# Two transformer blocks on one core: the dilated layers' values as products of 512 columns

## The chip, the cores and the metric

The kernel runs on one core of one Trainium2 chip. The metric is the device time of one execution in microseconds; several executions are timed and the median is compared. Every matrix product is made in three parts in a 32-bit format: an operand is split into a high part and a low part, and high x high, low x high and high x low are added up in PSUM.

## The reference

The input is 512 tokens of 1024 features. `first_block` runs two layers, `second_block` one.

```python
def first_block(x, ...):
    for layer in range(2):
        h = rms_norm(x, norm_g[layer])
        p = h @ w_in[layer]
        c_q, c_kv, k_r, gate_a, dil_qkv, gate_b = jnp.split(p, split_points, axis=-1)
        a = mla_attention(c_q, c_kv, k_r, ...) * jax.nn.silu(gate_a)
        b = dilated_attention(dil_qkv, cos_d, sin_d) * jax.nn.silu(gate_b)
        x = x + jnp.concatenate([a, b], axis=-1) @ w_out[layer]
    return rms_norm(x, final_g)
```

`dil_qkv` holds queries, keys and values (8 heads of 64) for three groups with dilations 1, 4 and 16. Each group attends within a band of its strided tokens; the three outputs are merged with weights from their sums of exponentials. `second_block` is a feed-forward stage (1024 to 2816 and back), a mixer (recurrence, sliding-window attention, gates), and a second feed-forward stage, each followed by a norm and a residual.

## The kernel before, in words

**Weight chunks.** All weights pass through one pipeline of chunks of 2048 columns per partition, two slots deep. SP loads a chunk into `WS` (`load`, L860), ScalarE copies it to its high part `WH` (`hi_of_chunk`), VectorE subtracts to get the low part `WL` (`lo_of_chunk`), TensorE multiplies. A slot of `WH` and `WL` comes free when the products of the chunk two before it are done. During an attention the chunk after next is split by the Pool engine instead (`split_in`). `make_plan` (L232) lists chunks and results in order and gives every wait its count; the order itself is written out by hand in each engine's program.

**Two forms of product.** `feature_major` (L1015) holds 128 x 128 of a weight and streams 512 tokens: 8 k-steps x 2 tiles x 3 parts = 48 products of 512 columns a chunk. `token_major` (L1053) holds 128 tokens' features and streams a weight's row of 256 columns, so that the result has tokens on the partitions: 8 x 4 x 3 = 96 products of 256 columns. The values (`v`) of the dilated attention are made in this form. They are 1536 columns wide: three groups g, two halves hh of the heads, 256 columns each; so six chunks in each layer.

**One layer.** For each half hh the chunks come in `DILATED_ORDER` (L225): q0, k0, v0, q1, k1, q2, k2, v1, and then the attention with eight items, for which `attention` (L1111) issues the scores of two items, then a filler chunk (here v2, on banks 6 and 7), then for every item scores, turning of the probabilities, and the products with values. ScalarE copies a values chunk out of PSUM in four blocks, scaled by the tokens' inverse norm (`from_token_major`, L1605). Group 0's values must be regrouped by residue of the token number. The Pool engine's queue writes them to DRAM and loads them back in 12 pieces (L926 to L938); value products of the first item wait for `v0_in`. The last turning and value products of an attention (`rest`) are issued between the first steps of the next chunk.

After the second half's attention come the gate chunks gb0 and gb1, then in0, in1, in2 (the latent columns) and ga0, ga1 (gates of the other attention). Between these chunks `weights_spread` (L1359) turns the merging weights of four pairs of heads with eight transposes each; VectorE makes the weights (`merge`, L2250, `weights_copy`, L2269) and applies them (`combine`, L2276).

**The start.** The input is loaded in four parts, each followed by the matching parts of chunks 0 and 1. TensorE turns each input part into a pair of banks (`input_turned`), ScalarE copies it to `X` and from `X` makes the high part with the gain (L1830, L1603), VectorE the low part (L2128); products of the first two chunks follow part by part (`first_step`). Between, `idle_products` (L1082) multiplies constants, so that TensorE is not idle.

**The passages.** After the first feed-forward stage and after the mixer, a norm over the whole result is needed before anything else: sums of squares (`norm_sum`, L1078), the root on ScalarE, the reciprocal on VectorE, a spread by four transposes (`norm_spread`, L1101), then residual and split. Three idle products stand before the spread, seven behind it (each two instructions of 128 columns at L1085).

Of the kernel before, what the change touches and what calls it, by code (L numbers as in the profile page):

```python
# [25 lines left out]
F32 = mybir.dt.float32  # L26
# [198 lines left out]
DILATED_ORDER = [("q", 0), ("k", 0), ("v", 0), ("q", 1), ("k", 1), ("q", 2), ("k", 2), ("v", 1)]  # L225
# [6 lines left out]
def make_plan():  # L232
# [3 lines left out]
    for L in range(DEPTH):  # L236
        pl.split(("x", L), KD)
        pl.norm(("x", L), KD)
        for hh in range(2):
            for w, g in DILATED_ORDER:  # L240
                if (w, g, hh) == ("v", 0, 0) or (w, g) == ("v", 1):
                    pl.aside((w, L, hh, g), "a", 3)
                    pl.add_chunk((w, L, hh, g), KD, CW, (w, L, hh, g))
                    continue
                pl.gemm((w, L, hh, g), "a" if w == "v" else "d")
                if w != "v":
                    pl.rope[w, L, hh, g] = len(pl.rope) + 1
            pl.attention(("dil", L, hh), [dict(kind="dil", L=L, t=t, j=2 * hh + jj, hh=hh, jj=jj)
                                          for jj in range(2) for t in range(NT)],
                         lambda: pl.filler(("v", L, hh, 2), "a"))  # L250
        for j in range(2):
            pl.gemm(("gb", L, j), "d")
        for j in range(3):
            pl.aside(("wb", L, j), "d", 3)
            pl.gemm(("in", L, j), "d")
# [91 lines left out]
def build_program(nc, a, out):  # L347
# [3 lines left out]
    with ctx:  # L351
# [76 lines left out]
        VD = ARENA[:, 6144:6144 + 3072].rearrange("p (g t c) -> p g t c", g=GROUPS, t=NT)  # L428
        OUN = view(9216, 4, 2, S)
# [85 lines left out]
        first_in = [sem(f"first_in{f}") for f in range(4)]  # L515
# [57 lines left out]
        v0_in = sem("v0_in")  # L573
        rls_ready = sem("rls_ready")
# [48 lines left out]
        def chunk_source(key):  # L623
            kind = key[0]
            if kind in ("in", "ga", "q", "k", "v", "gb", "uq", "ukv", "wo"):
                L = key[1]
                w = a["w_in"][L]
                if kind == "in":
                    return cols(w, key[2] * CW)
                if kind == "ga":  # L630
                    return cols(w, COL_GA + key[2] * CW)
                if kind in "qkv":
                    hh, g = key[2:]
                    return cols(w, COL_DIL + (3 * g + "qkv".index(kind)) * HEADS * HD + hh * CW)
# [15 lines left out]
        def landing(c):  # L650

            return 16 * (c // 2)

        def staged(c, columns):

            return THIRD[:, 0:columns] if c == 2 else WS[:, c % 2, 0:columns]

# [74 lines left out]
        def value_products(it):  # L732
# [10 lines left out]
            elif it["kind"] == "dil":  # L743
                for block in range(NT):
                    for b in range(2):
# [4 lines left out]
                        got.append((dst, 4 * b + block, VD[:, g, tile, h * HD:(h + 1) * HD],  # L750
# [44 lines left out]
        filler_of.update({("dil", L, hh): ("v", L, hh, 2) for L in range(DEPTH) for hh in range(2)})  # L795
# [37 lines left out]
        def _(sp):  # L833
            for f in range(4):
# [3 lines left out]
                for c in range(2):  # L838
                    sp.dma_start(slot(WS, c, KD, CW)[:, 2 * f:2 * f + 2, :],
                                 chunk_source(pl.chunks[c][0])[:, 2 * f:2 * f + 2, :]).then_inc(first_in[f], 16)  # L840
# [2008 lines left out]
```

## Time and profile before

| | us |
|---|---|
| median of 3 runs | 2117.63 |
| lowest, highest | 2116.81, 2117.83 |
| the profiled execution | 2117.32 |
| its span, first to last instruction | 2115.5 |
| TensorE busy in the span | 2099.6 |
| VectorE, ScalarE, Pool busy | 1135.1, 804.9, 121.8 |

The profile's rows come from one execution. Times on the left of a timeline row count from the span's start; a row of the timeline gives start, duration, engine, source line, operation, output and input, shape and count, and in brackets the idle time before it and what ended it. Products overlap in TensorE, so a product's own duration (0.28 or 0.39 us) is longer than the time from one start to the next.

### The profile page before, as it was taken

The page shows a single profiled execution, that of the slowest core. Times are in us where ns is not written, and L with a number is a line of the kernel's source. Part 1 is how long each engine was busy: PE and PEld are TensorE (multiplying, and loading weights), DVE is VectorE, ACT ScalarE, POOL GpSimd, SP SyncE. Part 2 cuts the span into 40 slices and gives each one's busy share as a digit, 9 for nine tenths or more (in the row PEclk, how much of TensorE's full clock was granted, in tenths as well). Part 3 has the DMA queues.
Part 4 walks back from the last instruction along what each step waited for, and adds up shares of the span by engine and source line. Part 5 has one row for each costly group of instructions (what it writes and reads, how often), then busy time and mean ns, then how long its engine had stood idle before and what let it go on. Part 6 is the DMA issues. An engine that isn't in the chain of part 4 may idle for free.

```text
span 2115.5 us, 28304 instructions
## 1 busy us (share of the span) xinstructions
PE 2099.6 (99%) x11655; PEld 1745.4 (83%) x11655; DVE 1135.1 (54%) x1543; ACT 804.9 (38%) x1296; POOL 121.8 (6%) x113
## 2 busy tenths in 40 slices
PE   8999999999999999999999999999999999999998
PEld 7888988788988887788888888787788888888886
DVE  6565557746555557664444435875643445333333
ACT  5152425723332526543122226463632245222223
POOL 0111100201001100200000002001000001000001
PEclk9999999999999999999999999999999999999999
DMA  5414212123323121123332224234023322333221
GB/s 189 120 41 120 81 60 82 41 61 101 100 58 105 59 79 64 41 80 99 99 99 86 99 95 149 86 116 138 12 90 100 100 80 90 99 99 99 100 99 60
DMA packets 158097, 189.03 MB, mean 89 GB/s; under 512 B 4194, under 2 KB 147876, under 8 KB 157860
## 3 DMA queue, kind: packets, MB, share of 16 engines
q1 hardware_dynamic: 153204, 174.41, 26.1%
q0 software_dynamic: 4608, 13.00, 2.0%
q8 instruction: 80, 1.31, 0.3%
q14 instruction: 29, 0.24, 0.0%
q10 hardware_dynamic: 176, 0.07, 0.0%
HBM read 182.20 MB, written 7.36 MB: 90 GB/s over the span
## 4 chain that ended last, share of the span: by engine, by line
PE 97%; DVE 1%; ACT 1%; issue 0%; DMA 0%; SPq 0%; DVEq 0%; ACTq 0%
PE PS L997 27%; PE PS L999 26%; PE PS L998 26%; PE PS L1126 5%; PE PS L1169 4%; PE PS L1138 4%; PE PS L1009 1%; PE PS L1005 1%; PE PS L1006 1%; PE PS L1078 0%; PE PS L1295 0%; DMA ARENA<-in_x 0%; PE PS L1369 0%; PE PS L1101 0%; DVE WL L2067 0%
## 5 line engine op out<-in xcount | busy, mean ns | idle before, releaser
L997 PE MATMUL PS<-UH,WH 128*128 128x512 f32 x1632 | 641.2, 393 | 0.1
L999 PE MATMUL PS<-UH,WL 128*128 128x512 f32 x1632 | 635.6, 389 | 0.0
L998 PE MATMUL PS<-UL,WH 128*128 128x512 f32 x1632 | 635.4, 389 | 0.0
L1566 ACT ACTIVATE WH<-WS 128x2048 fp32r<-128x2048 f32 x98 | 187.9, 1917 | 609.1 <-PE PS L999 587.6
L997 PEld LDWEIGHTS PS<-UH,WH 128*128 128x128 f32 x1632 | 306.4, 188 | 68.1 <-issue 6.1
L999 PEld LDWEIGHTS PS<-UH,WL 128*128 128x128 f32 x1632 | 306.3, 188 | 64.7
L998 PEld LDWEIGHTS PS<-UL,WH 128*128 128x128 f32 x1632 | 306.5, 188 | 61.5
L2067 DVE TENSOR_TENSOR WL<-WS,WH 128x2048 fp32r<-128x2048 f32 x98 | 224.3, 2289 | 234.4 <-ACT WH L1566 234.4
L2356 DVE TENSOR_TENSOR WL<-WS,WH 128x2048 fp32r<-128x2048 f32 x44 | 100.7, 2288 | 150.8 <-ACT WH L1739 150.8
L1739 ACT ACTIVATE WH<-WS 128x2048 fp32r<-128x2048 f32 x44 | 84.4, 1918 | 248.9 <-PE PS L999 246.6
L997 PE MATMUL PS<-WH,UH 128*128 128x256 f32 x416 | 118.3, 284 | 0.2 <-DVE WL L2067 0.2
L998 PE MATMUL PS<-WL,UH 128*128 128x256 f32 x416 | 117.7, 283 | 0.0
L999 PE MATMUL PS<-WH,UL 128*128 128x256 f32 x416 | 117.7, 283 | 0.0
L1138 PE MATMUL PS<-IDN,PR 128*128 128x128 f32 x624 | 85.7, 277 | 1.3 <-DVE PT L2212 0.3
L1169 PE MATMUL PS<-PT,ARENA 128*64 128x128 f32 x1248 | 85.8, 279 | 0.0
L1138 PEld LDWEIGHTS PS<-IDN,PR 128*128 128x128 f32 x624 | 69.6, 140 | 16.0 <-issue 7.2
L997 PEld LDWEIGHTS PS<-WH,UH 128*128 128x128 f32 x416 | 79.8, 192 | 2.2 <-DVE ARENA L2136 0.8
L998 PEld LDWEIGHTS PS<-WL,UH 128*128 128x128 f32 x416 | 79.8, 192 | 0.3
L999 PEld LDWEIGHTS PS<-WH,UL 128*128 128x128 f32 x416 | 79.8, 192 | 0.0
L1169 PEld LDWEIGHTS PS<-PT,ARENA 128*64 128x64 f32 x1248 | 66.5, 136 | 14.3 <-issue 14.3
L2212 DVE COPY PT<-PS 128x512 f32<-128x512 f32 (+1 forms) x80 | 53.7, 672 | 33.5 <-PE PS L1138 33.5
L997 PE MATMUL PS<-HH,WH 128*128 128x512 f32 x176 | 68.5, 389 | 0.0
(320 smaller groups left out, 3091.4 us busy)
## 6 DMA issues: line engine op xcount, KB each, us to landing
WS<-in_ffn_w SPq DMA_DIRECT2D x66, 1024.0 KB, 5.2
WS<-in_w_in SPq DMA_DIRECT2D x61, 1024.0 KB, 5.4
WS<-in_w_out SPq DMA_DIRECT2D x8, 1024.0 KB, 5.2
WS<-in_w_gate SPq DMA_DIRECT2D x8, 1024.0 KB, 5.3
WS<-in_w_attn_out SPq DMA_DIRECT2D x4, 1024.0 KB, 5.5
WS<-in_w_lru_out SPq DMA_DIRECT2D x4, 1024.0 KB, 5.4
WS<-in_w_o SPq DMA_DIRECT2D x4, 1024.0 KB, 5.1
bias_skewed<-bias_rows POOLq DMA_DIRECT2D x1, 3072.0 KB, 13.4
```

The source lines that it names most:

```text
L997: nc.tensor.matmul(dst, sh, mh, start=start, stop=False, skip_group_check=True)
L998: nc.tensor.matmul(dst, sh, ml, start=False, stop=False, skip_group_check=True)
L999: return nc.tensor.matmul(dst, sl, mh, start=False, stop=stop, skip_group_check=True)
L1005: nc.tensor.matmul(dst, sh, mh, start=start, stop=False, skip_group_check=True)
L1126: last[b] = nc.tensor.matmul(acc[:, c0:c0 + w], q, k, start=start, stop=True, skip_group_check=True)
L1138: last = nc.tensor.transpose(bank(4 + b)[:, k * P:(k + 1) * P], PR[:, n % 2, b * S + k * P:b * S + (k + 1) * P], IDN[:, :])
L1169: last = nc.tensor.matmul(dst, v, PT[:, n % 2, k * P:(k + 1) * P], start=start, stop=stop, skip_group_check=True)
L1566: nc.scalar.activation(WH[:, c % 2, 0:kt * n], staged(c, kt * n), ACT.Copy).then_inc(w_hi, 1)
L1739: nc.scalar.activation(WH[:, c % 2, :], WS[:, c % 2, :], ACT.Copy).then_inc(w_hi, 1)
L2067: tt(WL[:, c % 2, 0:kt * n], staged(c, kt * n), WH[:, c % 2, 0:kt * n].bitcast(F32), ALU.subtract).then_inc(w_split, 1)
L2212: nc.vector.tensor_copy(used_half(it, PT[:, n % 2, 0:S]), used_half(it, bank(4))).then_inc(pt_dve, 1)
L2356: tt(WL[:, c % 2, :], WS[:, c % 2, :], WH[:, c % 2, :].bitcast(F32), ALU.subtract).then_inc(w_split, 1)
```

## The change

- **Values.** The six values chunks of a layer become six half-row chunks of the same size: 4 of the 8 k-steps, 512 columns, namely two blocks of 256 side by side. `vv` is groups 0 and 1 of one half hh, `vw` is group 2 of both halves; each has two chunks (part 0 and part 1 of the k-steps). `value_half` streams 512 columns into banks 4 to 7, one bank for each tile of tokens, in the order 2, 3, 0, 1; the accumulation runs over both chunks. ScalarE's `values_out` copies eight blocks after the second. Group 2 of the second half is kept in a place of its own, `VDB`.
- **Order.** First half: q0, k0, vv, vv, q1, k1, q2, k2, vw, vw. Second half: q0, k0, q1, k1, q2, k2, vv, vv. The filler of the dilated attentions is a gate chunk (gb1, then gb0) instead of a values chunk; VectorE takes it out by a multiply.
- **Round trip.** In the first half Pool's queue does it as before, in the second half SP's queue (`by_residues`), once blocks (0, 0) to (0, 3) are copied.
- **Behind the second half.** in0 follows at once, with `rest` between its steps; the spreads of in1 and in2 stand between their steps.
- **Start.** One idle run of 7 on constants before any load; ScalarE makes the high part straight from the turned tile, VectorE the low part too, and `X` is copied afterwards. The weight parts of chunks 0 and 1 have a semaphore and a place each. Input part 1 is turned after the first two steps of chunk 0, not before them.
- **Passages.** Idle products of 512 columns, 4 before the spread and 9 behind it. The norm of the second layer's input is summed one step later.

```diff
-DILATED_ORDER = [("q", 0), ("k", 0), ("v", 0), ("q", 1), ("k", 1), ("q", 2), ("k", 2), ("v", 1)]
+DILATED_ORDER = ([("q", 0), ("k", 0), ("vv", 0), ("vv", 1), ("q", 1), ("k", 1), ("q", 2), ("k", 2),
+                  ("vw", 0), ("vw", 1)],
+                 [("q", 0), ("k", 0), ("q", 1), ("k", 1), ("q", 2), ("k", 2), ("vv", 0), ("vv", 1)])
...
+            def by_residues(L):
+                sp.wait_ge(w0_here, L + 1)
+                sp.dma_start(VSCR.rearrange("(i r) c -> i r c", r=NT), VRES).then_inc(w0_out, 16)
+                sp.wait_ge(w0_out, 16 * (L + 1))
+                for r in range(NT):
+                    of_r = VSCR.rearrange("(i r) c -> r i c", r=NT)[r]
+                    sp.dma_start(VD[32 * r:32 * r + 32, 0, 0:3, :], ...).then_inc(w0_in, 16)
+                    for x in range(2):
+                        sp.dma_start(VD[p0:p0 + 16, 0, 3, :], ...).then_inc(w0_in, 16)
...
+                if key[0] == "gb" and key[2] == 0:
+                    load(c, chunk_source(pl.chunks[c][0]))
+                    c += 1
+                    load(c, chunk_source(pl.chunks[c][0]))
+                    c += 1
+                    by_residues(key[1])
...
+            def value_half(w, L, hh, part):
...
+                for k in range(KD // 2):
+                    for t in (2, 3, 0, 1):
...
+                        tok = slice(t * P, (t + 1) * P)
+                        row = KD // 2 * part + k
+                        last = three(bank(4 + t), UH[:, row, tok], UL[:, row, tok], slot(WH, c, KD // 2, 2 * CW)[:, k, :],
+                                     slot(WL, c, KD // 2, 2 * CW)[:, k, :], row == 0, row == KD - 1)
+                last.then_inc(acc_ready, 1)
...
+            def wide_idle_products(n, of):
+                for _ in range(n):
+                    nc.tensor.matmul(bank(5), of[:, 0:P], of, start=True, stop=True, skip_group_check=True)
...
+                    if n == n0 and kind == "dil":
+                        pe.wait_ge(act_out, pl.act_out["vv" if it["hh"] else "vw", it["L"], it["hh"], "all"])
...
-                    idle_products(3, bank(5)[:, 0:P])
+                    wide_idle_products(4, HH[:, 0, 0, :])
                     norm_spread((f, "post"))
-                    idle_products(7, bank(5)[:, 0:P])
+                    wide_idle_products(9, HH[:, 0, 0, :])
...
+            pe.wait_ge(const_ok, 1)
+            idle_products(7, bank(3)[:, 0:P], ONES)
...
             input_turned(0)
             idle_products(4, bank(3)[:, 0:P])
-            input_turned(1)
-            idle_products(3, bank(3)[:, 0:P])
...
-                    if c == 0 and k < 4:
-                        input_turned(2 + k // 2)
+                    if c == 0 and k < 6:
+                        input_turned(1 + k // 2)
...
+                    def gate_beside():
+                        pe.wait_ge(act_out, pl.act_out[values_of, L, hh, "two"])
+                        feature_major(("gb", L, 1 - hh))
...
-                for j in range(2):
-                    feature_major(("gb", L, j), between=rest if j == 0 else None)
+                feature_major(("in", L, 0), between=rest)
                 weights_spread(L, 0)
-                feature_major(("in", L, 0))
-                weights_spread(L, 1)
-                feature_major(("in", L, 1))
-                weights_spread(L, 2)
-                feature_major(("in", L, 2))
+                feature_major(("in", L, 1), between=lambda k: weights_spread(L, 1) if k == 5 else None)
+                feature_major(("in", L, 2), between=lambda k: weights_spread(L, 2) if k == 2 else None)
                 weights_spread(L, 3)
...
                     for f in range(4):
+                        first_weights_hi(f, 0)
                         ready(("xt", f))
+                        for k in (2 * f, 2 * f + 1):
+                            nc.scalar.activation(UH[:, k, :], pair(("xt", f))[:, k % 2, :], ACT.Copy,
+                                                 scale=gain_of(("x", L), k)).then_inc(hi_done, 1)
+                        first_weights_hi(f, 1)
...
+                def values_out(w, hh):
+                    ready((w, L, hh, 1))
+                    dsts = (VRES, VD[:, 1, :, :]) if w == "vv" else (VD[:, 2, :, :], VDB)
+                    for x, t in ((0, 2), (1, 2), (0, 3), (1, 3), (0, 0), (0, 1), (1, 0), (1, 1)):
+                        ins = nc.scalar.activation(dsts[x][:, t, :], bank(4 + t)[:, x * CW:(x + 1) * CW], ACT.Copy,
+                                                   scale=RC[:, 2, t:t + 1])
...
-                    attention(("dil", L, hh))
+                    attention(("dil", L, hh), lambda: by_rms(("gb", L, 1 - hh), GB[:, 2 - 2 * hh:4 - 2 * hh, :]))
```

## Rows read from the trace of the kernel before

**Rows 1.** The page, busy us, share of the span and instructions.

```profile
PE 2099.6 (99%) x11655; PEld 1745.4 (83%) x11655; DVE 1135.1 (54%) x1543; ACT 804.9 (38%) x1296; POOL 121.8 (6%) x113
```

**Rows 2.** TensorE's waits: engine, line, waited for, us in total, times, longest.

```profile
PE PS L1303 <- DMA PR<-in_norm_g: 4.5, 1, 4.5
...
PE PS L1138 <- DVE PT L2212: 0.3, 1, 0.3
```

**Rows 3.** Timeline of TensorE, a dilated values chunk, first and last product.

```profile
218.37 0.28 PE L997 MATMUL PS<-WH,UH 128*128 128x256 f32 x1
...
229.76 0.28 PE L999 MATMUL PS<-WH,UL 128*128 128x256 f32 x1
```

**Rows 4.** Timeline of TensorE, last feed-forward stage.

```profile
2000.06 0.39 PE L997 MATMUL PS<-WH,HH 128*128 128x512 f32 x1
...
2010.26 0.39 PE L997 MATMUL PS<-WH,HH 128*128 128x512 f32 x1
```

**Rows 5.** Timeline of ScalarE, the copies of a values chunk.

```profile
230.08 1.57 ACT L1610 ACTIVATE ARENA<-PS,RC 128x256 f32<-128x256 f32 x4 [9.54 <-PE PS L999]
```

**Rows 6.** Timeline of TensorE, then VectorE, behind the sliding window's filler.

```profile
1468.80 0.60 PE L1138 MATMUL PS<-IDN,PR 128*128 128x128 f32 x4
...
1469.07 1.23 DVE L2136 TENSOR_TENSOR ARENA<-PS,RI 128x1024 f32<-128x1024 f32 x1 [1.19 <-PE PS L999]
1470.21 0.41 DVE L2212 COPY PT<-PS 128x256 f32<-128x256 f32 x1
```

**Rows 7.** Timeline of TensorE behind a dilated attention's filler.

```profile
243.58 1.03 PE L1138 MATMUL PS<-IDN,PR 128*128 128x128 f32 x8
...
246.66 1.09 PE L1169 MATMUL PS<-PT,ARENA 128*64 128x128 f32 x16
```

**Rows 8.** The round trip: Pool's queue, landings of L929 and L933, an SP issue.

```profile
180.13 0.58 POOL L933 DMA_DIRECT2D ARENA<-dil_values  x1 [2.65 <-DMA dil_values<-ARENA]
...
185.32 0.99 POOL L937 DMA_DIRECT2D ARENA<-dil_values  x2
...
DMA to landing us min/median/max: 2.9/3.7/5.9
...
DMA to landing us min/median/max: 2.4/3.4/5.3
...
13.45 0.30 SPq L854 DMA_DIRECT2D PR<-in_ffn_pre_g  x1
```

**Rows 9.** Timeline of VectorE, behind the second half's attention.

```profile
276.10 1.29 DVE L2273 COPY ARENA<-WGT 128x1024 f32<-128x1024 f32 x2
277.97 1.22 DVE L2136 TENSOR_TENSOR ARENA<-PS,RI 128x1024 f32<-128x1024 f32 x1 [0.58 <-PE PS L999]
```

**Rows 10.** Timeline of TensorE, the start.

```profile
5.04 1.97 PE L1315 MATMUL PS<-IDN,ARENA 128*128 128x128 f32 x8 [0.30 <-DMA ARENA<-in_x]
6.80 1.92 PE L1085 MATMUL PS<-ONES,IDN 128*128 128x128 f32 x8
...
10.62 0.47 PE L997 MATMUL PS<-UH,WH 128*128 128x512 f32 x1
...
13.45 1.03 PE L1315 MATMUL PS<-IDN,ARENA 128*128 128x128 f32 x8
```

**Rows 11.** Timeline of ScalarE and of VectorE, the start.

```profile
6.61 1.15 ACT L1824 ACTIVATE WH<-WS 128x512 fp32r<-128x512 f32 x2 [3.46 <-DMA WS<-in_w_in]
...
8.71 1.34 ACT L1603 ACTIVATE UH<-X,G 128x512 fp32r<-128x512 f32 x2
...
9.54 1.42 DVE L2128 SCALAR_TENSOR_TENSOR UL<-X,G,UH 128x512 fp32r<-128x512 f32 x2 [0.98 <-ACT UH L1603]
```

**Rows 12.** The passages: a stretch with its clock (PEclk), then TensorE's spreads.

```profile
1299.54:1302.95 3.41, 3.41 (x18) 3.41 (x18) 2.18 (x4) 2.14 (x5) 0.00 (x0) 0.50 0.00 0
...
1299.60 1.06 PE L1101 MATMUL PS<-IDN,RC 128*128 128x128 f32 x4
...
1739.12 0.65 PE L1101 MATMUL PS<-IDN,RC 128*128 128x128 f32 x4
```

More of the change, by code:

```diff
@@ L624, in chunk_source @@
             kind = key[0]
-            if kind in ("in", "ga", "q", "k", "v", "gb", "uq", "ukv", "wo"):
+            if kind in ("in", "ga", "q", "k", "vv", "vw", "gb", "uq", "ukv", "wo"):
                 L = key[1]
                 w = a["w_in"][L]
+                if kind in ("vv", "vw"):
+                    hh, part = key[2:]
+                    rows = w[part * S:(part + 1) * S]
+                    heads = ((0, hh), (1, hh)) if kind == "vv" else ((2, 0), (2, 1))
+                    return [cols(rows, COL_DIL + (3 * g + 2) * HEADS * HD + h * CW) for g, h in heads]
                 if kind == "in":
@@ L650, in landing, with half_of @@
         def landing(c):
-            return 16 * (c // 2)
+            return sum(32 if key[0] in ("vv", "vw") else 16 for key, *_ in pl.chunks[c % 2 + 2:c + 1:2])
         def staged(c, columns):
             return THIRD[:, 0:columns] if c == 2 else WS[:, c % 2, 0:columns]
+        def half_of(t, x):
+            return t.rearrange("p (k x n) -> p x k n", k=KD // 2, x=2)[:, x]
         def first_part(t, c, f):
@@ L1065, in token_major @@
                 last.then_inc(acc_ready, 1)
+            def value_half(w, L, hh, part):
+                c = pl.chunk[w, L, hh, part]
+                weights(c)
+                if part == 0:
+                    if w == "vw":
+                        pe.wait_ge(act_out, pl.act_out["vv", L, 0, "all"])
+                        if L == 0:
+                            pe.wait_ge(small_dve, 3)
+                    elif hh or L:
+                        past = pl.item_at["dil", L, 0][1] if hh else pl.item_at["mla", L - 1][1]
+                        results_taken(past)
+                        pe.wait_ge(pt_dve, past)
+                        pe.wait_ge(pt_act, past)
+                    else:
+                        pe.wait_ge(act_out, pl.act_out["xt", 3])
+                for k in range(KD // 2):
+                    for t in (2, 3, 0, 1):
+                        if (w, hh, part, k) == ("vv", 0, 0, 0) and t < 2:
+                            pe.wait_ge(*((inv_copied, pl.copied["x", L]) if t == 0 else (small_dve, 2)))
+                        tok = slice(t * P, (t + 1) * P)
[3 more added lines that the diff above has]
+                last.then_inc(acc_ready, 1)
             def norm_sum(name, kt):
@@ L1843, in _ @@
                 hi_of_chunk(c0 + 3)
[L1845 to L1846 removed]
+                def values_out(w, hh):
[4 more added lines that the diff above has]
+                                                   scale=RC[:, 2, t:t + 1])
+                        if t == 1 or (x, t) == (1, 3):
+                            if x:
+                                took((w, L, hh, "all" if t == 1 else "two"), ins)
+                            elif w == "vv" and hh:
+                                ins.then_inc(w0_here, 1)
                 for hh in range(2):
[L1849 removed]
+                    for i, (w, g) in enumerate(DILATED_ORDER[hh]):
                         key = (w, L, hh, g)
[L1851 to L1852 removed]
+                        if w in ("vv", "vw") and g == 1:
+                            values_out(w, hh)
                         if hh == 1 or i > 1:
```

181 lines of the change are left out of this document (89 added, 92 removed).

## The prediction

> **What bounds the kernel now.** I read the page first, its busy times: TensorE is busy 2099.6 us of the span of 2115.5 us [rows 1]. Whatever another engine saves is therefore worth nothing unless TensorE was waiting for it. So I asked next for TensorE's waits: the longest after the first load (4.5 us) are below one microsecond, and all seven lines of that view together hold 6.9 us; the last row shows what such a line looks like [rows 2]. TensorE is the bound in every stage but the first ten microseconds and the two passages between the big stages, and time can only come from fewer or denser products there. The page cannot say how dense they are, since busy times of overlapping products are run together. The starts of products in the timeline can: in a dilated value chunk, products of 256 columns start from 218.37 to 229.76 us, 95 steps of 119.9 ns [rows 3]; in the last feed-forward stage, products of 512 columns in the same roles (tokens' features held, weights streamed) start from 2000.06 to 2010.26 us, 45 steps of 226.7 ns [rows 4]. Two narrow products cost 239.8 ns and the wide one that computes the same costs 226.7: 13.1 ns a pair.
>
> **The values as wide products.** Before, each layer has six value chunks of 8 x 4 x 3 = 96 products, 12 chunks and 1152 products in both layers. After, each layer has three groups of two half-row chunks, each of 4 x 4 x 3 = 48 products of 512 columns: 576 in all. Every one of them takes the place of two narrow ones. 576 x 13.1 ns = 7.5 us less, all on the engine that sets the end. There are still 20 weight chunks of 2048 columns in this stage of a layer, so splitting them and loading them costs what it did. Against this speaks the Trainium skill (TensorE: Matmul & The Clock Gate, Back-to-back issue gap), which gives a gap of columns / 2.4 plus 2.5 ns: by it a pair would save only 2.5 ns, and the sum of this part would be an estimated 1.4 us. The trace disagrees at both widths: 119.9 and 226.7 ns are 13.2 and 13.4 ns over their columns at 2.4 GHz [rows 3, 4]. I take the trace.
>
> **ScalarE around it.** It now takes eight blocks of 256 columns after a pair of chunks where it took four in 1.57 us [rows 5], so about 3.0 us. Where it is next needed, after the first pair, the copies are followed by a chunk's high part (1.9 us) and VectorE's low part (2.3 us): 7.2 us inside a product chunk of 48 x 0.2267 = 10.9 us. Before an attention, the maxima and exponentials of the first two items come 1.45 us later, inside the gate chunk of 10.9 us that TensorE runs meanwhile. TensorE starts that gate chunk after four copies, as it did before. Cost: nothing; without the cover it would be 1.45 us at each of four attentions.
>
> **The gate as filler of the attentions.** VectorE, not ScalarE, now empties the filler's banks, with one multiply of 1.2 us ahead of its copy of the first turned item. The sliding-window attention already does this. There the multiply begins at 1469.07 and the copy at 1470.21, 0.27 and 1.41 us after the filler's end at 1468.80 [rows 6]. In the dilated attention the copy is of 512 columns (0.69 us), so it would end 2.10 us after the filler; with some 0.1 us for the signal, 2.2. TensorE wants it 2.06 us after: the second turning (1.02 us) starts ahead of 246.66, at 245.64, and the filler ended at 243.58 [rows 7]. I book +0.14 us at each of four attentions, +0.6; bounds 0 and, from the longest such step in the sliding window (0.3 us of waiting in the waits' view [rows 2]), +1.2. The waiting turn holds back only the products behind it in TensorE's queue.
>
> **Residues' round trip on SP's queue.** In the second half of the heads, group 0's values are computed last instead of early, go out to DRAM and come back in 12 pieces, now from SP's queue. Clock from the end of the last value product, T. The sixth copy ends at about T + 2.4 (six times 0.37 and the signal). Writing out lands 3.7 us after its issue, 5.9 at most; on the Pool queue the 12 issues then last from 180.13 to 186.30, 6.2 us, and a piece lands 3.4 us later, 5.3 at most [rows 8]. That makes T + 15.7 at this queue's pace. SP issued a small load in 0.30 us [rows 8], so I expect 12 issues in some 4 us and the last landing near T + 13.5. The data are wanted when the first item's value products start. Before, that was 246.66 - 229.88 = 16.8 us after T [rows 3, 7]; the filler shrinks by 0.6, so 16.2. No wait, booked at 0. Behind it SP's queue holds only the load of the chunk after next, needed more than 25 us later. The first half's trip stays with Pool, four chunks (over 40 us) ahead of its use. The copy weights for merging are ready at 276.10 + 0.65 = 276.8 us, and they are now wanted one chunk earlier, at the end of the chunk that ends at 277.9 [rows 9]: 1.1 us to spare, cost nothing; if merging were later by more, each layer would pay the excess. Spreads put between the steps of a chunk cost what they cost between chunks.
>
> **The start.** Today ScalarE splits both weight parts (from 6.61 us, after waiting for the load, 1.15), copies the turned input, then makes the high part (0.7), VectorE the low part (0.7), and the first product starts at 10.62 [rows 10, 11]. After, one weight part (0.6 us) stands ahead, the copy is behind and the high part is read from the turned tile: 6.61 + 0.6, high part to 7.9, low part to 8.65, first product near 8.7. The four idle products behind the first turning (6.80 + 1.92 = 8.72 [rows 10]) allow no earlier one. That gains 1.9 us. But the second turning (1.03 us [rows 10]) moves from ahead of the first product into the stream, where it now costs its time, and the products until about 9.3 us run at the lower clock, which loses another 0.3. Net 0.6. The seven idle products before any load use empty time; if they raise the clock sooner (eight turnings took 1.97 us at 5.04 and 1.03 at 13.45 [rows 10], so the level was half at the first), up to 1.0 more. I take -0.8, bounds -1.6 and +0.4.
>
> **The passages.** In the first passage the granted clock was 0.50 for 3.41 us, following norm sums and narrow idle products; the spread of the norm took 1.06 us there and 0.65 in the second passage, where it was still at full clock [rows 12]. Full clock would save 0.4 us of which the wider idle products ahead (4 x 0.227 us instead of 0.77) take back 0.14. In the second passage the dip came after the spread, and its first low product starts when VectorE is ready, so nothing is won. I take -0.2; bounds -0.4 (no extra delay) and +0.9: should the clock fall all the same, a wide idle product costs twice 0.227 us and thirteen of them run past what they fill, by some 0.4 us in the first passage and 0.5 in the second.
>
> **The sum.** -7.5 + 0.6 + 0 - 0.8 - 0.2 = -7.9 us. The profiled execution took 2117.32 us (span 2115.5 and 1.8 around it), so 2109.4 by its measure. The median of the runs, 2117.63, is 0.3 above it: forecast 2109.7 us. The bounds of the terms give, by the same addition, -9.5 and -5.0.
>
> **Rivals.**
> - *VectorE hands over late and the start gives nothing.* Each dilated attention loses 0.6 us, twice the sliding window's longest wait, because the multiply delays the maxima behind it as well, and the first product's gain is spent on the second turning. -7.5 + 2.4 + 0 - 0.2 = -5.3 us, 2112.3. For it speaks that the same pattern does stall today; against it that the maxima start only after the scores, at about the time the copy ends. Chance 0.14.
> - *Width pays nothing* (the change doesn't do what it says): the 13 ns go with columns, or switching among four banks at each group costs them. Then only -0.4 us remains, 2117.2. Against it stand the two paces, the wide one measured over all banks. By the page's gap above it would be near this too, an estimated 6.1 us short of my sum. Chance 0.05.
> - *The round trip is late*, the case that ends slower. The wait is TensorE's, at the first item's value products, twice in the kernel. With the worst hops of Pool's queue the trip takes 5.9 + 6.2 + 5.3 = 17.4 us [rows 8] where the slack is 16.2 - 2.4 = 13.8: 3.6 us at each of two attentions, and 0.7 us of the gain are left. From a trip of 17.8 us on the kernel is slower than before; if weight loads beside it on SP's queue stretch it to 20 us, it costs 2 x 6.2 and gives 2122.1. For it: a trip beside loads did take longer than the median; against: no weight load is due at that time. Chance 0.03, of which 0.02 ends slower.
> - The rest, 0.02, is no difference through something that no view shows.
>
> **How the numbers follow.** My forecast has 0.76; its own range is 2108.1 to 2112.7. The range for 8 in 10 is 2107.7 to 2112.6: the bounds of the forecast, a little lower on one side for a start that gains more than its row allows, with most of the first rival inside. About 0.2% (4.2 us, so 2113.4) is what a measurement of this kernel can tell from no change. Faster by more: forecast, first rival and no others, 0.90. Within: width, part of the round trip, the rest, 0.08. Slower: 0.02.
>
> **What would show it.** In the profile after: groups of 576/3 = 192 products of 512 columns at the value chunk's line, 227 ns from start to start, and 32 narrow ones of each kind left (the sliding window's); a pair of value chunks lasting 21.8 us; the first product at 8.0 to 8.8 us; TensorE's turn of the second item waiting 0.1 to 0.3 us for VectorE in four attentions; no wait for a load of the values from DRAM; the passages with or without a stretch at 0.50. Starts of wide value products over 235 ns apart, or a wait of over a microsecond for the residues or for the copied weights, would prove me wrong.

## The result, and the profile after

The changed kernel takes 2106.76 us (median of 5 executions, 2106.10 to 2107.76) against 2117.34 us (5 executions, 2116.81 to 2117.83) for the one before: ratio 0.9949, 95% interval 0.9938 to 0.9960. It is 10.6 us faster. The forecast was 7.9 us, 2109.7 us, and its range ended at 2107.7: the sign was right, the size was not, and 0.9 us lie outside the range. The profiled execution was the median one itself, with a span of 2105.0 us. Of the 2.9 us between 2109.7 and 2106.76, 0.3 is the kernel before itself, whose median was 2117.63 when the forecast was made.

First the page: its busy times, then the group of the value chunks.

```profile
PE 2093.7 (99%) x11073; PEld 1713.8 (81%) x11073; DVE 1134.7 (54%) x1543; ACT 804.9 (38%) x1296; POOL 108.3 (5%) x87
...
L1041 PE MATMUL PS<-WH,UH 128*128 128x512 f32 (+1 forms) x224 | 84.0, 375 | 0.2 <-issue 0.2
```

TensorE has 582 instructions fewer than in [rows 1]: 576 value products, and a net six of the idle ones and of the start. Pool has 26 fewer, 87 after 113, a number that the prediction read past. With forms kept apart, the value chunks' group falls into two:

```profile
L1041 PE MATMUL PS<-WH,UH 128*128 128x512 f32 x192 | 74.9, 390 | 0.2 <-issue 0.2
...
L1041 PE MATMUL PS<-WH,UH 128*128 128x256 f32 x32 | 9.2, 286 | 0.0
```

These are the 192 wide products of a kind and the 32 narrow ones (sliding window) that were foretold. The timeline of TensorE over the first pair of value chunks gives their pace, to set against [rows 3, 4]:

```profile
36.57 0.39 PE L1042 MATMUL PS<-WL,UH 128*128 128x512 f32 x1
...
57.68 0.39 PE L1042 MATMUL PS<-WL,UH 128*128 128x512 f32 x1
```

93 steps in 21.11 us are 227.0 ns each; in the four pairs behind a wide chunk it is 226.7. TensorE's waits, all but the last few lines, compared with [rows 2]:

```profile
PE PS L1155 <- POOL EPSC L943: 1.0, 1, 1.0
PE PS L1053 <- DVE UL L2197: 1.0, 2, 0.5
PE PS L1395 <- DMA ARENA<-in_x: 0.7, 1, 0.7
```

No load of values from DRAM and no copied weights are among them. So far the products. What was not foretold lies behind the last one. In the timeline of TensorE before the change the last product starts at 2107.27 us, and the span ends at 2115.5: 8.2 us. After:

```profile
2098.80 0.39 PE L1043 MATMUL PS<-WH,HL 128*128 128x512 f32 x1
```

Span end 2105.0, only 6.2 us later. The last product came 8.47 us sooner, the end 10.5 us sooner: 2.1 us of the gain are where no product is. SyncE's waits at the end of the program (L351, now L355, is where the kernel's block is opened and closed), before and after:

```profile
SPq L351 <- PEq L351: 2.3, 1, 2.3
SPq L351 <- DMA out<-ARENA: 1.7, 1, 1.7
```

```profile
SPq L355 <- DMA out<-ARENA: 1.7, 1, 1.7
...
SPq L355 <- PEq L355: 0.2, 1, 0.2
```

The wait for the last store is the same. What follows it is the engines' meeting at the block's end, and it shrank from 2.3 to 0.2 us. The releaser named is TensorE's queue, which cannot be: the instructions of that line (queue, operation; duration in ns; start in us) show who ended last (PEldq is TensorE's queue of weight loads). Before:

```profile
L351 PEldq DRAIN  x1: 4267/4267/4267, 2103.4 to 2103.4; - x1
L351 POOLq DRAIN  x1: 7602/7602/7602, 2107.7 to 2107.7; - x1
...
L351 DVEq DRAIN  x1: 1455/1455/1455, 2109.6 to 2109.6; - x1
...
L351 SPq DRAIN  x1: 13/13/13, 2113.2 to 2113.2; - x1
```

TensorE's drain ended at 2103.4 + 4.3 = 2107.7, VectorE's at 2111.0, SyncE's (behind the last store) at 2113.2, Pool's at 2107.7 + 7.6 = 2115.3. Pool's closing DRAIN set the end. After:

```profile
L355 POOLq DRAIN  x1: 5479/5479/5479, 2099.2 to 2099.2; - x1
...
L355 SPq DRAIN  x1: 13/13/13, 2104.7 to 2104.7; - x1
```

It takes 5.48 us, ends at 2104.69, and the store's landing and it end together. The drain begins while Pool still works on its last two sums (of result and residual, one after the other):

```profile
2098.58 2.50 POOL L1023 TENSOR_TENSOR ARENA<-ARENA 128x512 f32<-128x512 f32 x2 [0.18 <-DVE ARENA L2496]
```

They end at 2101.1, 1.9 us after the drain's start, and it is the same 1.9 us before the change and in run 3. The change took 26 DMAs off Pool (two layers, 13 each: one write and 12 reads of the second half's trip), and 2.12 us / 26 = 0.082 us for each.

The pair of traces, by the starts of equal products, gives this ledger. To the end of the first two chunks -0.71 us; from there to the first passage -7.45; first passage (from its sums of squares to the next stage's first product) -0.34; from there to the last product +0.02; behind it -2.1. Sum -10.6. Of the -7.45, -7.25 are accounted for below (values -7.7, handovers +0.45); 0.2 were not traced.

### The profile page after: what moved, and what is told of

Same layout as the page of the kernel before. It is cut to its first block, busy times and chain, and to the rows that moved or that the text cites. A ratio compares the mean times of both kernels' runs of the same rounds, so it can differ in the third digit from the quotient of the medians.

```text
span 2105.0 us, 27147 instructions
## 1 busy us (share of the span) xinstructions
PE 2093.7 (99%) x11073; PEld 1713.8 (81%) x11073; DVE 1134.7 (54%) x1543; ACT 804.9 (38%) x1296; POOL 108.3 (5%) x87
## 3 DMA queue, kind: packets, MB, share of 16 engines
q0 software_dynamic: 3424, 10.90, 1.7%
## 4 chain that ended last, share of the span: by engine, by line
PE 98%; ACT 1%; DVE 1%; issue 0%; DMA 0%; DVEq 0%; ACTq 0%
PE PS L1041 27%; PE PS L1043 27%; PE PS L1042 27%; PE PS L1202 5%; PE PS L1247 4%; PE PS L1216 4%; PE PS L1053 1%; PE PS L1050 1%; PE PS L1049 1%; PE PS L1148 1%; PE PS L1373 0%; PE PS L1447 0%; PE PS L1177 0%; PE PS L1395 0%; DMA ARENA<-in_x 0%
## 5 line engine op out<-in xcount | busy, mean ns | idle before, releaser
L1041 PE MATMUL PS<-WH,UH 128*128 128x512 f32 (+1 forms) x224 | 84.0, 375 | 0.2 <-issue 0.2
L1042 PE MATMUL PS<-WL,UH 128*128 128x512 f32 (+1 forms) x224 | 83.8, 374 | 0.0
L1043 PE MATMUL PS<-WH,UL 128*128 128x512 f32 (+1 forms) x224 | 83.7, 374 | 0.0
L1042 PE MATMUL PS<-HL,WH 128*128 128x512 f32 x176 | 68.5, 389 | 0.0
L1041 PE MATMUL PS<-WH,HH 128*128 128x512 f32 x176 | 68.5, 389 | 0.0
L1042 PE MATMUL PS<-WL,HH 128*128 128x512 f32 x176 | 68.5, 389 | 0.0
L1043 PE MATMUL PS<-HH,WL 128*128 128x512 f32 x176 | 68.5, 389 | 0.0
```

What stands on the lines that cost most here:

```text
L1041: nc.tensor.matmul(dst, sh, mh, start=start, stop=False, skip_group_check=True)
L1042: nc.tensor.matmul(dst, sh, ml, start=False, stop=False, skip_group_check=True)
L1043: return nc.tensor.matmul(dst, sl, mh, start=False, stop=stop, skip_group_check=True)
```

## The experiments

The theory after the result: the width gives what was booked; the excess is Pool's drain, which grows by the DMA. Rivals: the drain grows with packets or bytes, or the second halves' trips on Pool had cost something elsewhere. The start and the passages, with small and uncertain terms, are tested by themselves. The runs came in three jobs, each on one chip with the kernel before beside them: runs 1, 2, 3 and 5, where before took 2117.23 us; runs 4, 6 and 7, 2117.12; runs 8 to 10, 2117.30. A difference from the change's 2106.76 us goes across jobs. In comparisons of products, "the middle" is the time from TensorE's first product of the norm's sums (behind the first two chunks) to its last product: 2075.68 us before, 2067.92 after.

**1. All trips back on Pool** (the changed kernel).

```
-                    by_residues(key[1])
...
-                    if hh:
-                        split_in(("dil", L, hh))
-                        continue
-                    pool.wait_ge(act_out, pl.act_out["vv", L, 0, "all"])
+                    ready_, out_, in_ = (w0_here, w0_out, w0_in) if hh else (act_out, v0_out, v0_in)
+                    pool.wait_ge(ready_, L + 1 if hh else pl.act_out["vv", L, 0, "all"])
```

> The changed kernel, with the second halves' round trips issued from the Pool queue again (69 DMAs issued by Pool in all instead of 43). Theory (Pool's closing drain takes time for every DMA it has issued): the last product stays where it is in the changed kernel, 2098.8 us, or up to 0.5 us later for a late trip; Pool's drain lasts 7.6 us again instead of 5.5, and the time is 2.0 us above the changed kernel's, near 2108.8. Rival 1 (the shorter end was chance): 2106.8. Rival 2 (the late round trip would stall on Pool's queue): waits for the loads from DRAM before the first value products, up to 2 us each, and the last product later by that.

Measured: 2109.10 us (2108.05 to 2109.84), ratio 0.9958 (0.9944 to 0.9971). Drain and last wait:

```profile
L355 POOLq DRAIN  x1: 7602/7602/7602, 2099.5 to 2099.5; - x1
```

```profile
SPq L355 <- PEq L355: 2.3, 1, 2.3
```

The middle is 2068.09 us, 0.17 from that of the change; the 2.3 us are behind the last product. A late trip, the case of the prediction that ended slower, did not come about even on Pool's slower queue: TensorE has no wait for these loads.

**2. The kernel before, with the second halves' trips on SP's queue.**

```
+            def by_residues(L):
+                sp.wait_ge(act_out, pl.act_out["v", L, 1, 0])
+                sp.dma_start(VSCR.rearrange("(i r) c -> i r c", r=NT), VRES).then_inc(w0_out, 16)
...
+                    if hh:
+                        split_in(("dil", L, hh))
+                        continue
```

> The kernel before, with nothing changed but the second halves' round trips, issued from SP's queue (43 DMAs by Pool instead of 69). Theory: all products stay in their places, the last one starts at 2107.3 us, and the time falls by 2.1 us to 2115.2, since Pool's drain lasts 5.5 us. Rival (chance, or something else in the new order shortens the end): no difference, 2117.3.

Measured: 2115.17 us (11 executions, 2114.72 to 2115.89), ratio 0.9989 (0.9980 to 0.9998), span 2113.4, 2.1 below that of before:

```profile
L351 POOLq DRAIN  x1: 5479/5479/5479, 2107.7 to 2107.7; - x1
```

So 2.1 us of the gain have nothing to do with the products. Moving 26 DMAs to another queue brings them alone.

**3. All four trips on SP's queue** (the changed kernel; Pool then issues 17 DMAs).

```
-            def by_residues(L):
+            def by_residues(L, hh=1):
...
+                if key[0] == "q" and key[2:] == (0, 2):
+                    by_residues(key[1], 0)
```

> The changed kernel with all four round trips on SP's queue (17 DMAs issued by Pool). Theory: Pool's drain falls to some 3.4 us and no longer ends last; the end is then set by the landing of the last output, 0.15 us before the drain's end in the changed kernel, so the time is 0.1 to 0.2 us less, 2106.6. Rival (the drain is part of every end): another 2.1 us less, 2104.7.

Measured: 2106.57 us (2106.09 to 2107.11), ratio 0.9946 (0.9933 to 0.9960).

```profile
L355 POOLq DRAIN  x1: 3360/3360/3360, 2099.6 to 2099.6; - x1
...
L355 SPq DRAIN  x1: 13/13/13, 2105.1 to 2105.1; - x1
```

The drain is shorter by another 2.1 us and nothing is gained: it now ends at 2102.9, and the last store at 2105.1 sets the end. The gain from this source has a floor, and the change reached it.

**4. What a DMA is to the drain: 26 tiny ones, and one of many pieces** (the changed kernel, at the start of Pool's program).

```
+            for i in range(26):
+                pool.dma_start(EXTRA[i:i + 1, 0, :], ONES[0:1, 0:16]).then_inc(extra, 16)
```

> The changed kernel with 26 more DMAs issued by Pool at the start, each one row of 64 bytes to a scratch tensor in DRAM; the number of Pool's DMAs is then 69, as in the kernel before, while their bytes and packets hardly grow. Theory (Pool's closing drain grows by the DMA, 0.082 us each, whatever a DMA carries): drain 7.6 us instead of 5.48, SyncE's last wait for the other engines 2.3 us instead of 0.2, time +2.1 us, about 2108.9 us. Rival (the drain grows with bytes or packets): drain about 5.5 us, time unchanged at 2106.8 us.

```
+            pool.dma_start(EXTRA[:, :, 0:12], ONES[:, 0:120].rearrange("p (a b) -> p a b", a=10)).then_inc(extra, 16)
```

> The changed kernel with one more DMA issued by Pool at the start, of 1280 pieces of 48 bytes, about as many packets as the 26 moved DMAs had (1184). Theory (by the DMA): drain +0.08 us, from 5.48 to 5.56 us, which is still within what the landing of the last output covers but for 0.1 us: time unchanged, 2106.8 us. Rival (by the packet): drain about 7.6 us, time +2.1 to +2.3 us, about 2109 us.

Measured: 2109.06 us (2107.81 to 2109.26) with the 26, 2106.27 us (2105.94 to 2107.32) with the one. Pool's drain and the page's row of its queue (packets, MB), for the 26 tiny ones:

```profile
L355 POOLq DRAIN  x1: 7604/7604/7604, 2099.4 to 2099.4; - x1
```

```profile
q0 software_dynamic: 4256, 10.90, 1.7%
```

and for the one of 1280 pieces:

```profile
L355 POOLq DRAIN  x1: 5562/5562/5562, 2098.8 to 2098.8; - x1
```

```profile
q0 software_dynamic: 3472, 10.96, 1.7%
```

Bytes are out: 26 DMAs with no bytes to speak of lengthen the drain as much as the moved trips with 2.1 MB. Packets are out too, though not by the run that was meant for it: the one DMA of 1280 pieces shows up as only 48 packets more (3472 after 3424), so it could not tell the two apart. The tiny ones do it: 4256 packets with 69 DMAs drain in 7604 ns, and the first run's 4608 packets with 69 DMAs in 7602. By the number of DMAs four points lie on one line: 17, 43, 44 and 69 DMAs, 3360, 5479, 5562 and 7602 ns, that is 1.97 us + 0.0816 us each, within 5 ns. They were issued some 2000 us before the drain in the tiny case, so it is not that they were still under way. Pool's instructions rise one for one with its DMAs (61, 87, 88 and 113), so these runs do not part a cost for each DMA from a cost for each instruction that issues one.

**5. Narrow value products** (the changed kernel, each wide product as two of 256 columns).

```
+                        for x in range(2):
+                            at_x = slice(x * CW, (x + 1) * CW)
+                            last = three(bank(4 + t)[:, at_x], UH[:, row, tok], UL[:, row, tok],
```

> The changed kernel with each value product of 512 columns made as two of 256, all else as it is. Theory (13.1 ns a pair): 576 more products, 7.5 us more, 2114.3, and 120 ns from start to start. Rival (order, filler and start carry part of the gain, width less): under 6 us more.

Measured: 2114.64 us (10 executions, 2113.36 to 2115.17), ratio 0.9984 (0.9975 to 0.9994). A pair of value chunks has 192 steps of 120.0 ns, 23.0 us, where the change has 96 of 226.7, 21.8 us. From the first to the last stretch with such chunks the run falls back by 7.71 us against the change (0.55 ahead in the start, 7.16 behind shortly before the first passage): 576 x 13.4 ns. Then another 1.16 us are lost in the first passage, where the two traces differ by their clock. A window of this run (the last three columns: granted clock, DMA share, GB/s) and TensorE's timeline there, and then the same two views of the changed kernel:

```profile
1298.00:1301.40 3.40, 3.40 (x11) 2.71 (x12) 1.04 (x4) 1.88 (x4) 0.00 (x0) 0.50 0.00 0
```

```profile
1299.55 1.05 PE L1180 MATMUL PS<-IDN,RC 128*128 128x128 f32 x4
1300.26 2.86 PE L1163 MATMUL PS<-HH 128*128 128x512 f32 x9
```

```profile
1291.00:1294.40 3.40, 3.37 (x17) 2.44 (x15) 2.19 (x5) 2.36 (x6) 0.00 (x0) 1.00 0.00 0
```

```profile
1291.68 0.60 PE L1177 MATMUL PS<-IDN,RC 128*128 128x128 f32 x4
1292.04 2.33 PE L1160 MATMUL PS<-HH 128*128 128x512 f32 x9
```

The wide idle products were in place in both, and in one of them the clock was at 0.50 (1.2 GHz) nonetheless. They then cost about double, as the prediction's bound had it, and push the first product of the next stage back.

**6. The old idle products in the passages** (the changed kernel).

```
-                    wide_idle_products(4, HH[:, 0, 0, :])
+                    idle_products(3, bank(5)[:, 0:P])
```

> The changed kernel with the old idle products (3 and 7 of 128 columns) in the two passages instead of 4 and 9 of 512. Theory (they were worth what the first passage lost at half clock, the 0.3 us that the two traces differ by there, and nothing in the second): +0.3 us where the clock falls in the first passage and 0 where it does not, about 2107.0 us. Rival (the wide ones carry a stretch of full clock that the narrow ones lose on every execution): +1.0 us or more, with a stretch of half clock after the first passage.

Measured: 2106.30 us (2105.72 to 2107.46), ratio 0.9950 (0.9937 to 0.9964). The medians show no loss, and the rival of +1.0 us is out. Its profiled execution kept the full clock through both passages. Over the profiled executions of all kernels here, the first passage had a stretch of 3.4 us at 0.50 in 4 of 10 with the wide idle products and in 1 of 4 with the narrow ones (which is before's own; run 2, the same passage in the same kernel but for two trips, had none). This window of run 2 stands against [rows 12]:

```profile
1299.54:1302.95 3.41, 2.74 (x24) 2.54 (x23) 2.42 (x6) 2.62 (x6) 0.00 (x0) 1.00 0.00 0
```

The stretch itself tells more than the medians. TensorE from the sums of squares to the next stage's first product, in the changed kernel and then in this run, both at full clock:

```profile
1289.78 1.03 PE L1148 MATMUL PS<-ONES,SQ 128*128 128x1 f32 x8
...
1294.64 0.47 PE L1049 MATMUL PS<-UH,WH 128*128 128x512 f32 x1 [0.26 <-ACT UH L1668]
```

```profile
1288.85 1.03 PE L1148 MATMUL PS<-ONES,SQ 128*128 128x1 f32 x8
...
1293.45 0.47 PE L1049 MATMUL PS<-UH,WH 128*128 128x512 f32 x1 [0.79 <-ACT UH L1668]
```

That is 4.86 against 4.60 us. At full clock it is 4.84 to 4.87 in all six profiles with the wide idle products and 4.60 in all three with the narrow ones, and the 0.25 us are still there nearly 100 us further on. The spread starts 1.9 us after the first sum where it started 1.64, since the four wide products ahead of it last longer. So at full clock the wide idle products cost 0.25 us.

With the dip the stretch takes 5.20 us in before and 5.98 to 6.02 in the four profiles with the wide ones. In three of these four the dip came when the spread had begun; the next low product, which otherwise waits for VectorE, then waits less, and 0.1 to 0.3 us of loss are left nearly 100 us further on. In run 5 the dip came ahead of the spread and 1.2 us are left; in before it was under way at the spread as well, and left 0.5. In the second passage before's dip cost nothing, as the first low product there starts when VectorE is ready. So what the passage costs hangs on an event that comes in some executions and not in others, and on where it falls; what the wide idle products do to it is a loss of 0.25 us that the medians cannot tell.

**7. The old start** (the changed kernel).

```
-            pe.wait_ge(const_ok, 1)
-            idle_products(7, bank(3)[:, 0:P], ONES)
...
+            input_turned(1)
+            idle_products(3, bank(3)[:, 0:P])
...
-                        act.wait_ge(lo_done, pl.lo[("x", L), 2 * f + 1])
```

> The changed kernel with the old start (first turns of the input, first parts of weights and input in the old order, no wide products before them). Theory (the start was worth what the end of the first two chunks' products moved, 31.59 to 30.89 us): +0.7 us, all of it before 31 us, about 2107.5 us. Rival (the gain comes back at the first wait behind, for loads or for VectorE): less than 0.2 us.

Measured: 2108.15 us (2107.76 to 2108.39), ratio 0.9958 (0.9944 to 0.9971). That is 1.4 us over the change, twice what I expected; against the unedited kernel of run 8 it is 0.8, against run 6 of the same job 1.9. None of it came back at a later wait: the middle is 2068.21 us. The next run shows why.

**8. The changed kernel once more.**

> The changed kernel once more, not edited. Theory (when the clock comes to full speed in the start differs from execution to execution, 4.4 to 9.3 us after the span's start in the runs so far, and the first products move with it): median 2106.3 to 2106.8 us, single executions from 2105.7 to 2107.8 us, and in the profiled one the product after the first two chunks' sums at 30.0 to 31.1 us. Rival (the start is fixed and the runs' edits moved it): 30.9 us again.

Measured: 2107.37 us (2106.12 to 2107.59), ratio 0.9952 (0.9939 to 0.9966). The median lies 0.6 us above the interval that I gave, so that part of the theory missed, and 0.6 us over the first job's: that much lies between two jobs of one kernel, so of the runs here nothing under it is told apart. The profiled execution, 2106.12 us, is the fastest of its five. TensorE's start in it, and then in the changed kernel's first profile:

```profile
4.87 1.10 PE L1395 MATMUL PS<-IDN,ARENA 128*128 128x128 f32 x8 [0.32 <-DMA ARENA<-in_x]
5.81 1.06 PE L1155 MATMUL PS<-ONES,IDN 128*128 128x128 f32 x8
7.95 0.50 PE L1041 MATMUL PS<-UH,WH 128*128 128x512 f32 x1 [1.09 <-DVE UL L2578]
...
30.01 0.27 PE L1148 MATMUL PS<-ONES,RB 128*128 128x1 f32 x1
```

```profile
5.26 1.97 PE L1395 MATMUL PS<-IDN,ARENA 128*128 128x128 f32 x8 [0.69 <-DMA ARENA<-in_x]
7.03 1.91 PE L1155 MATMUL PS<-ONES,IDN 128*128 128x128 f32 x8
8.80 0.51 PE L1041 MATMUL PS<-UH,WH 128*128 128x512 f32 x1
...
30.88 0.49 PE L1148 MATMUL PS<-ONES,RB 128*128 128x1 f32 x3
```

Here the eight turnings took 1.10 us, there 1.97: the clock was up at 4.4 us in the one and at 8.9 us in the other. The same code, the same work, 0.9 us apart at the end of the first chunks. Over all profiles the clock came up between 4.4 and 9.3 us with the new start (ten profiles, mean 7.1) and between 9.3 and 11.2 with the old (four, mean 10.3); the sums' first product stood at 29.96 to 31.14 us, mean 30.52, and at 31.59 to 32.34, mean 32.02. The start is worth 1.5 us on average. The two traces that I had compared first showed 0.7, because before's was the earliest of its four and the change's among the late of its ten.

**9. The filler behind the first turned block**, in the changed kernel, and the same with all trips on SP's queue.

```
-                if filler:
+                if filler and mla:
...
+                    if n == n0 and filler and not mla:
+                        filler()
```

> The changed kernel with VectorE's filler multiply put behind the first turned block instead of ahead of it, in the dilated and the sliding-window attentions. Theory (the first turn waits for VectorE because the filler is ahead of the block it needs, 0.11 us more in each of the four dilated attentions than in the kernel before): the gap between scores and first turn falls by 0.1 us or more in each, about -0.6 us in all, 2105.8 us. Rival (that gap is TensorE's own handover from scores to turns and VectorE is in time anyway, or the gain is given back at the values): less than 0.2 us.

> The changed kernel with all four trips of values by residue on SyncE's queue and the filler behind the first turned block, as in the run with the filler alone. Theory: the filler's gain alone, about -0.6 us, since the end is set by the landing of the last output and not by Pool's drain (3.4 us with 17 DMAs): 2105.8 us. Rival (the two add up): 0.2 us or more below the run with the filler alone.

Measured: 2107.11 us (2105.84 to 2108.10) and 2106.35 us (2105.98 to 2107.25), ratios 0.9951 (0.9938 to 0.9965) and 0.9948 (0.9934 to 0.9961). TensorE in the first dilated attention, in the changed kernel:

```profile
139.64 1.06 PE L1216 MATMUL PS<-IDN,PR 128*128 128x128 f32 x8
...
145.90 0.55 PE L1216 MATMUL PS<-IDN,PR 128*128 128x128 f32 x3
```

and with the filler behind:

```profile
138.88 1.09 PE L1216 MATMUL PS<-IDN,PR 128*128 128x128 f32 x8
...
145.34 0.44 PE L1216 MATMUL PS<-IDN,PR 128*128 128x128 f32 x2
```

The step from the last score to this turning falls from 313 to 202 ns, as in the kernel before; the theory has its place right. But two turnings on, 6.46 us have passed instead of 6.26: the multiply now delays the maxima (VectorE began them 0.32 us after the turning, where it was at once), and the 0.1 us and as much again is paid there. The middle is 2068.26 us, against 2067.92. The rival holds: given back. Neither version beats the change; the second is inside its spread.

**10. The wide values alone**: the changed kernel with the edits of runs 1, 6 and 7 together.

> The changed kernel with the old start, the old idle products and all trips on Pool: of the change only the wide value products, with what their order of loads and parts needs, are left. Theory (the parts add up: values -7.5, handovers +0.45, start 0, end 0): -7.1 us, about 2110.1 us, Pool's drain 7.6 us. Rival (the parts depend on each other, or something that no part has gives or takes time): off by more than 0.5 us from that.

Measured: 2110.44 us (6 executions, 2109.72 to 2110.77), ratio 0.9966 (0.9954 to 0.9978), 6.9 us less than the 2117.30 of before in the same job. Expected were 7.1. The parts add up: -6.9 here, -1.4 for the start (run 7), -2.1 to -2.3 for the drain (runs 1, 2 and 4) give -10.4 to -10.6; measured -10.6. With 0.6 us between two jobs of one kernel, the sum cannot show the 0.25 us of the passages.

## Why the prediction was off, point by point

- **The bound.** TensorE's products, right for all but the last 8 us of the span. The statement that time can only come from fewer or denser products was the flaw. The time after the last product was not read, and there the bound was Pool's queue.
- **The step that failed** is the last one: the sum was taken off the profiled execution's span as if the stretch behind the last product stayed as it was. The prediction moved the second halves' trip to SP's queue and counted its 13 issues there, but counted their leaving Pool at nothing. Before's trace had it all: Pool's drain of 7602 ns, a wait of 2.3 us that outlasts the one for the last store, 113 instructions on Pool. It could not give the price of a DMA in the drain; but bounds from 0 to the 2.1 us between Pool's drain and SyncE's would have held the result. Term missed: -2.1.
- **Values.** -7.5 booked, -7.7 measured (576 x 13.4 ns, run 5). Right. The gap in the Trainium skill (TensorE: Matmul & The Clock Gate, Back-to-back issue gap), by which this part would have been an estimated 1.4 us, does not hold here: the steps at both widths, 120.0 ns in run 5 and 226.7 in the change, are 13.3 and 13.4 ns over their columns at 2.4 GHz. The prediction also left out that the same section of the Trainium skill calls this the gap of an isolated product and gives about 131 ns at 512 columns for a stream of weight loads and products. The 226.7 ns measured do not agree with that either. The rival that width pays nothing fell with it.
- **VectorE's filler.** +0.14 at each of four attentions booked; 0.11 measured (313 ns after 203 at all four), +0.45 in all. Right, and the prediction named its place. The first rival, 0.6 at each, did not occur.
- **Round trip.** SyncE's timeline in layer 0, with the write, the first read and the last two reads, and then the landing times of the small pieces (L899):

```profile
250.43 0.35 SPq L891 DMA_DIRECT2D dil_values<-ARENA  x1
254.29 0.34 SPq L895 DMA_DIRECT2D ARENA<-dil_values  x1
...
258.87 0.89 SPq L899 DMA_DIRECT2D ARENA<-dil_values  x2
```

```profile
DMA to landing us min/median/max: 1.7/1.9/2.0
```

  The last of the reads is issued at 259.3 and lands near 261.3. The values ended at 247.9, so that is T + 13.4; forecast T + 13.5. TensorE's first value products of that half are at 264.17, T + 16.3; forecast T + 16.2. No wait. Two errors cancelled: the twelve issues took 5.5 us, 0.46 each, not some 4, and the pieces landed in 1.9 us, not 3.4. That the landing fell at the forecast time is luck.
- **Start.** -0.8 booked, within bounds -1.6 and +0.4; -1.5 measured on average. Mis-sized: the first product at 7.9 to 8.9 us was right, but the 1.0 us for an earlier clock was booked at a fifth, and the profile of before that the term was read off had the earliest first product of the four with the old start (10.62 us, the others 10.98 to 11.37). The clock came up 3.3 us sooner on average with the new start.
- **Passages.** -0.2 booked, as a full clock instead of the dip less 0.14 for the wider products ahead of the spread. The pair of traces has -0.3 there, but by luck: the wide products did not keep the dip away (it came in four of ten profiles), only in this one it stayed out. At equal, full clock they cost 0.25 us (run 6), so the step that a wider idle product holds the clock and so gains failed. For a clock that falls all the same in the first passage some +0.4 was allowed for; there the stretch to the next product grew by 0.8 us, 6.0 after before's 5.20; further on run 5 stood 1.0 us behind before's passage, the other three profiles with the dip by at most 0.1. The second passage, with +0.5 in that bound, had no dip in any of the ten profiles with the wide ones.
- **The range.** By the measured terms without the end, the passages at equal clock, -7.7 + 0.45 - 1.5 + 0.25 = -8.5 us, 2109.1 us, inside the range. The 2.1 us of the end put it outside. The chance of 0.9 for faster was borne out.

What stays open: why Pool's drain grows with DMAs long finished, whether it is the DMA or the instruction that issues it that counts, and what decides in a given execution whether the clock falls in the passages. The 1.97 us of the drain without any DMA are probably Pool's last two sums, which end 1.9 us after its start; no run moves them.

## What to carry to other kernels

Read the end of the span as a stage of its own: list each engine's last instruction, the closing drains too, and see which ends last; the releaser that the profile names for the final meeting may be one long done. When an edit moves DMAs from one queue to another, price both ends, the queue that loses them too. And before a term of under one microsecond is read off two traces, look whether the clock's rise or a dip differs between them: one kernel's own executions differ by as much. Where a stretch repeats from profile to profile, as the passage at full clock does within 0.03 us, compare it over all of them: it tells what the medians cannot.

## What the runs showed of the hardware that was not expected

- Pool's DRAIN at the end of a block took 3.36 us with 17 DMAs issued in the whole program, 5.48 with 43, 5.56 with 44 and 7.60 with 69: 0.082 us for each DMA, whatever its bytes or packets, and however long ago it landed.
- One DMA of 1280 pieces of 48 bytes added 48 packets to the queue's count; 26 DMAs of one 64-byte row added 832.
- The same program's clock reached full level at 4.4 us in one execution and at 8.9 us in another, and its passages ran with or without 3.4 us at half level. Idle products of 512 columns did not exclude that, and at full clock they made the passage 0.25 us longer.
